# High products first in a stage's opening tiles, conditioning pieces in runs of four, a rotation without TensorE

## The reference

```
def trunk(x, c, pos, past, p):
    silu_c = jax.nn.silu(c)
    for l in range(DEPTH):
        mod = (silu_c @ p['w_ada'][l] + p['b_ada'][l]).reshape(B, N_MOD, D)
        m = [mod[:, j][:, None, :] for j in range(N_MOD)]
        hh = modulate(rmsnorm(x, p['g_pre'][l, 0]), m[0], m[1])
        f = swiglu(hh, p['w_ffn_gate'][l, 0], p['w_ffn_up'][l, 0], p['w_ffn_down'][l, 0])
        x = x + 0.5 * m[2] * rmsnorm(f, p['g_post'][l, 0])
        ...
```

```
def rope(x, pos, inv_freq):
    half = inv_freq.shape[0]
    ...
    x1 = xf[..., :half]
    x2 = xf[..., half:rot]
    out = jnp.concatenate([x1 * cos - x2 * sin, x2 * cos + x1 * sin, xf[..., rot:]], axis=-1)
```

## Time and profile before

| | us |
|---|---|
| median of 3 runs | 1423.23 |
| lowest, highest | 1422.56, 1423.35 |
| the profiled execution | 1422.14 |
| its span | 1420.5 |
| PE busy in the span | 1357.0 |
| DVE busy | 789.7 |
| ACT busy | 613.5 |
| POOL busy | 87.5 |

### The profile page before, as it was taken

The page is one execution under the profiler, slowest core; times in us unless marked ns, Lnnn a source line. Parts: engine busy times, 40 slices in busy tenths (PEclk is TensorE's granted clock), DMA queues, the critical chain, the costliest instruction groups (busy, mean ns, idle before and its releaser), DMA issues.

```text
span 1420.5 us, 24392 instructions
## 1 busy us (share of the span) xinstructions
PE 1357.0 (96%) x9798; PEld 1256.7 (88%) x9798; DVE 789.7 (56%) x1446; ACT 613.5 (43%) x1043; POOL 87.5 (6%) x139
## 2 busy tenths in 40 slices
PE   5899999999999998999999899999989999999996
PEld 2799999979886697999999799999978888999996
DVE  1544444576697777444445743445567976444444
ACT  2534333444343455334344533334457755333342
POOL 0000000003001101000000100000011100000000
PEclk9799999999999999999999999999999999999998
DMA  9565655456249755564355556444466643444442
GB/s 364 209 210 197 205 178 187 147 199 227 90 160 341 258 210 208 180 205 151 120 163 163 206 179 207 163 135 138 159 242 224 224 163 106 148 148 150 129 150 83
DMA packets 82260, 260.08 MB, mean 183 GB/s; under 512 B 11634, under 2 KB 22962, under 8 KB 82034
## 3 DMA queue, kind: packets, MB, share of 16 engines
q1 hardware_dynamic: 65682, 199.56, 41.9%
q0 software_dynamic: 16480, 59.15, 12.0%
HBM read 254.45 MB, written 4.23 MB: 182 GB/s over the span
## 4 chain that ended last, share of the span: by engine, by line
PE 82%; DVE 10%; DMA 3%; ACT 3%; issue 2%; SPq 1%; DVEq 0%; ACTq 0%
PE ps L1614 25%; PE ps L1615 25%; PE ps L1616 25%; PE ps L1679 3%; DMA lent_lo<-in_ada 1%; DVE w_lo L2077 1%; DVE f L2159 1%; DVE x L2145 1%; DVE f L2165 1%; DVE f L2141 1%; DVE xn_lo L2153 1%; DMA x<-in_x 1%; PE ps L589 1%; DMA a_raw<-in_ada 1%; PE ps L1701 1%
## 5 line engine op out<-in xcount | busy, mean ns | idle before, releaser
L1614 PE MATMUL ps<-xn_hi,w_hi 128*128 128x320 f32 x1808 | 573.6, 317 | 21.6 <-DVE xn_lo L2153 18.2
L1616 PE MATMUL ps<-xn_hi,w_lo 128*128 128x320 f32 x1808 | 560.9, 310 | 0.0
L1615 PE MATMUL ps<-xn_lo,w_hi 128*128 128x320 f32 x1808 | 560.8, 310 | 0.0
L2077 DVE TENSOR_TENSOR w_lo<-w_raw,w_hi 128x1024 fp32r<-128x1024 f32 (+1 forms) x357 | 382.3, 1108 | 128.3 <-ACT w_hi L1884 127.7
L1614 PEld LDWEIGHTS ps<-xn_hi,w_hi 128*128 128x128 f32 x1808 | 341.4, 189 | 50.6 <-issue 29.6
L1884 ACT ACTIVATE w_hi<-w_raw 128x1024 fp32r<-128x1024 f32 x362 | 331.6, 961 | 88.8 <-PE ps L1616 78.3
L1615 PEld LDWEIGHTS ps<-xn_lo,w_hi 128*128 128x128 f32 x1808 | 341.7, 189 | 1.4
L1616 PEld LDWEIGHTS ps<-xn_hi,w_lo 128*128 128x128 f32 x1808 | 341.5, 189 | 0.0
L1614 PE MATMUL ps<-mid_hi,w_hi 128*128 128x320 f32 x704 | 218.3, 310 | 0.3 <-DVE w_lo L2077 0.3
L1616 PE MATMUL ps<-mid_hi,w_lo 128*128 128x320 f32 x704 | 217.3, 309 | 0.0
L1615 PE MATMUL ps<-mid_lo,w_hi 128*128 128x320 f32 x704 | 217.3, 309 | 0.0
(11 more groups left out here) (282 smaller groups left out, 962.1 us busy)
## 6 DMA issues: line engine op xcount, KB each, us to landing
w_raw<-in_gu SPq DMA_DIRECT2D x176, 512.0 KB, 4.5
a_raw<-in_ada POOLq DMA_DIRECT2D x96, 512.0 KB, 4.8
...
```

What stands on the lines that cost most here:

```text
L1614: pe.matmul(out, hi, xhi, start=start, stop=False)
L1615: pe.matmul(out, hi, xlo, start=False, stop=False)
L1616: return pe.matmul(out, w_lo[s][:, w_at:w_at + P], xhi, start=False, stop=stop)
L2077: dve.tensor_tensor(w_lo[s][:, cols], w_raw[:, s, cols], w_hi[s][:, cols].bitcast(F32), ALU.subtract).then_inc(w_split, 1)
```

## The change

It has four parts.

1. `two_tiles` and `both_blocks` no longer call `three_passes`. For a chunk, PE first does the two passes that read only `xn_hi` (`high_passes`, waiting for `xn_high`), for both banks; the pass that reads `xn_lo` (`low_pass`) follows one chunk later.
2. DVE's order at the boundaries before even_in, gate1, gate2, odd_in and gate3 goes chunk by chunk from chunk 2 on (`late_chunks`), and the two operations on the sample columns of chunks 2 to 7 are done by GpSimd, behind its eight loads and its half of a low part. gate0 keeps DVE's order.
3. The pieces within gate0, down0, gate1, gate2 and the odd tail stand in runs of four (one of five) in place of one per tile or block. The numbers of pieces per stage are the same.
4. The permutation product of blocks 10 to 17 goes. ACT copies the two halves of the block from PSUM into `rope_b` crosswise (two copies of 64x320) before its own copy, and DVE multiplies that with a sine table that carries the sign. Blocks 0 to 7 keep theirs.

```diff
-ADA_PLAN += [("gate0", c, 1 if c > 1 else 0) for c in range(FC)]
-ADA_PLAN += [("down0", m, 1 if m < 4 else 0) for m in range(KC)]
+ADA_PLAN += [("gate0", c, 4) for c in (3, 7, 11, 15, 19)] + [("down0", 1, 4)]
...
-ADA_PLAN += [("gate1", c, 1 if 6 <= c < 14 else 0) for c in range(FC)]
+ADA_PLAN += [("gate1", c, 4) for c in (8, 13)]
...
-ADA_PLAN += [("odd_tail", q, 2 if q == 5 else 1) for q in range(4, 2 * KC)] + [("odd_out", ("first", 2), 3)]
+ADA_PLAN += [("odd_tail", 5, 4), ("odd_tail", 10, 4), ("odd_tail", 13, 5)] + [("odd_out", ("first", 2), 3)]
...
             ada_load(gp, pieces[A_SLOTS:KC])
+            for k in range(2, KC):
+                samples(gp, stage, k)
+
+        def samples(gp, stage, k):
+
+            sub = PNORM[stage]
+            fs = tokens(f[:, k, PTOK:TOK])
+            gp.wait_ge(xr_ready, 8 * sub + k + 1)
+            gp.tensor_tensor(fs, fs, per_sample(modT[:, scale_at(sub, k), 1:NCOND]), ALU.mult).then_inc(scaled_s, 1)
+            gp.wait_ge(scaled_s, (KC - 2) * (sub - 1) + k - 1)
+            gp.tensor_tensor(fs, fs, per_sample(modT[:, shift_at(sub, k), 1:NCOND]), ALU.add).then_inc(xmod_ready, 1)
...
                 if b <= 9:
-                    rotate(b - 2, b - 2, 0)
-                elif B_RQK < b <= B_RQK + 8:
-                    rotate(b - 1, b - 1 - (B_RQK - 8), 1)
+                    rotate(b - 2, b - 2)
...
+                    if B_RQK <= b < B_RQK + 8:
+                        act.wait_ge(rope_done, CR + b + h - 3)
+                        for to, of in ((0, HD), (HD, 0)):
+                            last = act.activation(rope_b[to:to + HD, h, :], ps[of:of + HD, 2 * j + h, 0:TOK], kinds[h][0],
+                                                  scale=kinds[h][1])
+                        last.then_inc(crossed, 1)
...
+            def rotate_halves(b, par):
+
+                dve.wait_ge(p_evac, PB + b + 1)
+                src = proj[:, b, :]
+                dve.wait_ge(crossed, b - B_RQK + 1)
+                steps.did(dve.tensor_tensor(rope_b[:, par, :], rope_b[:, par, :], ropet[:, 3, :], ALU.mult))
+                steps.did(dve.tensor_tensor(src, src, ropet[:, 2, :], ALU.mult))
+                steps.wait()
+                dve.tensor_tensor(src, src, rope_b[:, par, :], ALU.add).then_inc(rope_done, 1)
...
+                for k in range(KC):
+                    high_of(0, k)
+                    if k:
+                        low_of(0, k - 1)
+                    if k >= behind:
+                        high_of(1, k - behind)
+                        low_of(1, k - behind)
+                low_of(0, KC - 1)
+                for k in range(KC - behind, KC):
+                    high_of(1, k)
+                    low_of(1, k)
...
+                def late_chunks():
+
+                    residual(2)
+                    scaled(2)
+                    low(1)
+                    residual(3)
+                    scaled(3)
+                    low(2)
+                    dve.wait_ge(w_split, CR + 2 * W_BASE[prep] + 3)
+                    ahead(prep, (1,))
+                    residual(4)
+                    scaled(4)
+                    low(3)
+                    for k in range(5, KC):
+                        grown(k)
+                        residual(k)
+                        scaled(k)
+                        low(k - 1)
+                    low(KC - 1)
```

More of the change, by code:

```diff
@@ L106 @@
 ADA_PLAN += into("gate1")
-ADA_PLAN += [("gate1", c, 1 if 6 <= c < 14 else 0) for c in range(FC)]
+ADA_PLAN += [("gate1", c, 4) for c in (8, 13)]
 ADA_PLAN += into("gate2")
-ADA_PLAN += [("gate2", c, 1 if 6 <= c < 14 else 0) for c in range(FC)]
+ADA_PLAN += [("gate2", c, 4) for c in (8, 13)]
 ADA_PLAN += into("odd_in")
-ADA_PLAN += [("odd_tail", q, 2 if q == 5 else 1) for q in range(4, 2 * KC)] + [("odd_out", ("first", 2), 3)]
+ADA_PLAN += [("odd_tail", 5, 4), ("odd_tail", 10, 4), ("odd_tail", 13, 5)] + [("odd_out", ("first", 2), 3)]
 ADA_PLAN += into("gate3")
@@ L126, in at_pieces @@
     return ADA_PIECES.get((stage, i), ())
[L129 removed]
+ADA_TURNS = {("front", 1): [0], ("front", 2): [1], ("gate0", 8): [2], ("gate0", 16): [3], ("down0", 2): [4],
              ("attention", 0): [5, 6, 7, 8, 9], ("gate1", 0): [10], ("gate1", 13): [11], ("gate2", 0): [12],
@@ L1616, in three_passes, with high_passes, low_pass @@
                 return pe.matmul(out, w_lo[s][:, w_at:w_at + P], xhi, start=False, stop=stop)
+            def high_passes(out, s, w_at, xhi, start):
+                pe.matmul(out, w_hi[s][:, w_at:w_at + P], xhi, start=start, stop=False)
+                pe.matmul(out, w_lo[s][:, w_at:w_at + P], xhi, start=False, stop=False)
+            def low_pass(out, s, w_at, xlo, stop):
+                return pe.matmul(out, w_hi[s][:, w_at:w_at + P], xlo, start=False, stop=stop)
             def w_half(n, h):
@@ L1624, in both_blocks, with low_of @@
                 w_half(W_BASE[stage], 1)
-                for i, k in enumerate(EVEN_OUT_ORDER if stage == "even_out" else range(KC)):
+                def low_of(i, k):
                     pe.wait_ge(xn_ready, 8 * PREP[stage] + i + 1)
                     for b in range(2):
-                        last = three_passes(ps[:, banks[b], 0:TOK], s, (b * KC + k) * P, xn_hi[:, k, :],
-                                            xn_lo[:, k, :], i == 0, i == KC - 1)
+                        last = low_pass(ps[:, banks[b], 0:TOK], s, (b * KC + k) * P, xn_lo[:, k, :], i == KC - 1)
                         if i == KC - 1 and b == 0:
                             last.then_inc(half_used, 1)
+                    return last
+                for i, k in enumerate(EVEN_OUT_ORDER):
+                    pe.wait_ge(xn_high, 8 * PREP[stage] + i + 1)
+                    for b in range(2):
+                        high_passes(ps[:, banks[b], 0:TOK], s, (b * KC + k) * P, xn_hi[:, k, :], i == 0)
+                    if i:
+                        low_of(i - 1, EVEN_OUT_ORDER[i - 1])
+                last = low_of(KC - 1, EVEN_OUT_ORDER[KC - 1])
                 return last
@@ L1637, in two_tiles, with low_of, high_of @@
                 hi, lo = (out_hi, out_lo) if stage == "odd_out" else (xn_hi, xn_lo)
-                order = [(0, k) for k in range(behind)]
-                for k in range(behind, KC):
-                    order += [(0, k), (1, k - behind)]
-                order += [(1, k) for k in range(KC - behind, KC)]
-                for y_, k in order:
+                def low_of(y_, k):
+                    if y_ == 0:
+                        pe.wait_ge(xn_ready, 8 * PREP[stage] + k + 1)
+                    for b in range(2):
+                        last = low_pass(ps[:, 2 * y_ + b, 0:TOK], (n + y_) % 2, (b * KC + k) * P, lo[:, k, :],
+                                        k == KC - 1)
+                        if k == KC - 1 and b == 0 and signal_half:
+                            last.then_inc(half_used, 1)
+                    if k == KC - 1:
+                        last.then_inc(w_used, 1)
+                def high_of(y_, k):
                     if k == 0 and stage == "odd_out":
@@ L2470, in tables @@
             for i in range(half):
-                perm[s + half + i, kind, s + i] = -1.0
-                perm[s + i, kind, s + half + i] = 1.0
+                if kind == 0:
+                    perm[s + half + i, s + i], perm[s + i, s + half + i] = -1.0, 1.0
             for o in (s, s + half):
                 rope[o:o + half, 2 * kind] = np.cos(ang)
-                rope[o:o + half, 2 * kind + 1] = np.sin(ang)
+                rope[o:o + half, 2 * kind + 1] = np.sin(ang) * (-1.0 if kind and o == s else 1.0)
     out["perm"], out["rope"] = perm, rope
```

45 lines of the change are left out of this document (17 added, 28 removed).

## The result

| | median us | runs |
|---|---|---|
| before | 1423.20 | 4, from 1422.56 to 1423.35 |
| after | 1406.78 | 4, from 1405.17 to 1408.10 |
| after, a second session | 1404.64 (before: 1422.49) | 4, from 1403.49 to 1405.28 |

The ratio after/before is 0.9885 (95% interval 0.9868 to 0.9902), in the second session 0.9873 (0.9858 to 0.9888): 16.4 and 17.9 us faster, where 22.9 were forecast. The range (1392 to 1410) held the time; the point was 6.5 us too low. The profiled execution took 1405.17 us.

What follows compares the result with a forecast made beforehand. PE was taken as the bound, with 82% of the chain. Terms 12.4 + 4.3 + 0.2 + 7.1 - 0.9 + 0.2 - 0.4 = 22.9 us gave a 1400.3 us median, range 1392 to 1410.

Steps and rivals of the forecast that it cites:

- Pieces in runs: In gates, down0 and the odd tail, each merged piece saves 0.34 us of PE: 10.2 plus 2.2, 12.4 us.
- The rotation: In blocks 10 to 17, eight products of PE go, saving 4.3 us, plus 0.2 in the attention stage.
- The first two tiles: At the stage boundaries, PE starts earlier and runs to tile 1's end without waits, 12.7 us instead of 15.1.
- gate0's -0.9: In gate0, PE arrives early at tile 1's weights, then meets the late tile 2 uncovered: 0.9 us lost.
- What becomes late next: Ahead of tile 2, `w_used` comes later relative to tile 1's end, so PE waits 0.85 us for weights.
- the resumption stays where it is: Behind the three pieces in even_in, gate1 and gate2, PE resumes no earlier; in odd_in 0.4 us earlier.
- GpSimd's price: Sample operations on GpSimd take 0.3 us each, 0.9 a pair, costing nothing unless a pair exceeds about 1.3.
- Rival C: GpSimd's operation costs 1.8 us or more, so five boundaries lose 47 us: 1454 us; chance 0.04.
- Rival B: GpSimd and DVE contend at five boundaries, DVE's chunk grows to 2.4 us, 9 us less gain: 1409; chance 0.14.
- Rival A: The boundaries give their whole wait back, pieces and tile 2's weights in time, 7.4 us more: 1393; chance 0.12.
- Rival D: A run's refill starves the weight loads, some 2.5 us late for each of 13 runs: 1432; chance 0.04.
- Rival E: Split high and low products cost PE 0.1 us at each of some 60 waits, 6 more: 1406; chance 0.08.

Runs made afterwards that it cites:

- the tiles alone: The kernel before with only the low part one step behind and the sample steps on GpSimd: 1417.74 us against 1423.44.
- the rotation alone: The kernel before with only the retention blocks' rotation done by copies on ACT: 1418.47 us against 1423.44.
- low_early: The changed kernel with tile 0's last low product moved ahead of tile 1's sixth step: 1399.74 us, in another session 1400.86.
- the pieces alone: The kernel before with only the pieces put in runs: 1412.52 us against 1423.44.
- filler: The changed kernel with idle products added on PE at gate2's boundary only: 1404.97 us against 1423.11 for the kernel before.
- odd_plain: low_early with the odd tail's thirteen pieces one by one as in the kernel before: 1402.21 us against 1423.00 for the kernel before.
- samples_dve: low_early with the sample steps of chunks 2 to 7 back on DVE: 1403.47 us against 1422.49 for the kernel before.
- pieces21: low_early with the third piece of the run behind chunk 1 moved ahead of chunk 4 at every boundary: 1398.98 us.
- ahead_early: pieces21 with DVE making the second half of tile 1's low weights before chunk 3's add: 1399.94 us.

## Why the prediction was right, and where it was off

- **Pieces in runs, 12.4.** Right in mechanism and near in size: 10.9 alone. 2.07 for four pieces, as worked out. The odd tail was mis-sized: 0.8 to 1.0, not 2.2, since ACT's `ra` and odd_out's first wait take 1.5 of the bound of 3.1. gate0 and down0 gave 5.0 of 6.1; of that last 1.1 the cause stays open, apart from 0.17 ahead of tile 2 and a start 0.27 later.
- **The rotation, 4.3 + 0.2.** Right: 5.0 (2.8 to 6.0), blocks 3.52 apart, ACT's copies covered. Its trace has 6.3 in the stretch from even_in to even_out; where the 1.8 above the forecast come from is open.
- **The first two tiles, 7.1 - 0.9 + 0.2 - 0.4 = 6.0.** The mechanism was right: 12.72 us from the resumption to tile 1's end. The sum was right alone (5.7), by luck, as its errors cancel. even_in was too low: I took 0.85 off for tile 2's weights, and none of these traces has a wait there. odd_in with odd_out was too high: 1.95 - 0.4 were forecast, 0.4 came. With the tiles alone the resumption there was 0.96 earlier, more than the 0.4 I counted, but 0.40 went to tile 1's low weights and 1.03 to the wait ahead of tile 2, and the wait ahead of odd_out's tile 2 grew from 0.46 to 1.63, 1.17 where I had taken 0.4. In the whole change even the 0.4 was gone, as the last piece's load was 1.04 late. gate0's -0.9 is neither shown nor refuted: the tiles alone read -1.0 there, but the rotation alone reads -1.4. gate3's 0.1 was too low by 1.8, for a load that landed earlier (the table above).
- **What becomes late next.** Right, with 0.68 in gate1 and gate2, 0.84 in gate3, 0.94 in odd_in and 1.05 in gate0 against 0.85. low_early shows its price: taking it away is worth about 5 us, and it was the change's own: tile 0's last low product had been put six passes later than it need be. I had worked out this wait and counted it as a cost only; the three lines that avoid it were the better use of the number.
- **What failed** are two things that the sum took as fixed. The first is that the terms add, each at full clock. At 2.4 GHz a pass is 0.147, and every term was priced so. From even_in on, 10.2 us at the lower level stand in both traces of the changed kernel, against 3.4 before: 3.4 us lost. Whether the change causes this is shown for neither place. At attention's end it was 6.8 us in both of these traces and with the pieces alone, 3.4 with the tiles alone and in filler (the changed kernel's program up to there), and in low_early 3.4 in one trace and none in the other. gate2's fall stands in both traces of the changed kernel and in no trace of a part alone, but again in odd_plain's.
- **The second** is that in even_in, gate1 and gate2 "the resumption stays where it is", and comes 0.4 earlier in odd_in. Against that it came later by 0.2, 0.3, 1.4 and 0.7 in the first trace of the changed kernel (0.0, 1.25, 1.1 and 0.5 in the second), 2.6 and 2.8 in sum. In gate2 and odd_in the tiles alone did not show this (11.21 and 9.98). The time of a DMA's landing was a term of the sum, set to no change without a bound.
- **GpSimd's price.** Taken as 0.3 an operation, 0.9 a pair; measured 0.45 and 0.34, and about 1.0 a pair: the pair stays under the 1.3 that would be seen. Rival C, with 1.8 or more an operation, is out.
- **Rival B**, contention: half right in kind, not in size. At each boundary one residual add, chunk 3's, which runs beside both sample steps of chunk 2, lasts longer. DVE and GpSimd in the changed kernel's gate2:

```profile
777.96 0.48 DVE L2199 TENSOR_TENSOR x<-x,f 128x320 f32<-128x320 f32 x1
...
779.28 0.58 DVE L2199 TENSOR_TENSOR x<-x,f 128x320 f32<-128x320 f32 x1
```

```profile
779.05 0.47 POOL L536 TENSOR_TENSOR f<-f,modT 128x64 f32<-128x64 f32 x1 [3.64 <-DVE f L2213]
779.60 0.42 POOL L538 TENSOR_TENSOR f<-f,modT 128x64 f32<-128x64 f32 x1
```

0.10 more, and over all 48 adds the mean went from 482 to 497 ns, 0.7 us in all. In samples_dve, with no sample step on GpSimd, no add took more than 0.494. The low parts, which also read two operands from SBUF, were not longer: at most 0.495, as before. The Trainium skill (GPSIMD Engine Reference, Key points) says that GpSimd contends with VectorE instructions that have two SBUF inputs. By that rule the adds agree in kind and the low parts show nothing of it; rival B's 9 us the traces refute. The time that rival B gave, 1409, is nearer to the first median (1406.78) than mine, for another reason.
- **Rival A** (1393): its conditions were not met, as every boundary waits for the pieces' loads. **Rival D**: ACT waits 83 us for PE to free its weight slots, and for the load of a weight tile only twice, 6.1 us in all (5.7 before), both ahead of the first tile and of any run. **Rival E**: passes go on at 0.147 over the new waits; the 86 passes of gate1 in 12.72 us leave no room for a bubble at each.

The fastest kernels found are low_early, pieces21 and ahead_early, 22 to 24 us under before and not to be told apart. low_early is the changed kernel and three lines.
